# The queries' rotary columns, dealt by halves to two stationary tiles in the second stage

## What is computed

```python
def rope(x):                       # d = 32 columns, angle = position * inv
    x1, x2 = xf[..., : d // 2], xf[..., d // 2:]
    return concat([x1 * cos - x2 * sin, x2 * cos + x1 * sin])

q = (rms_norm(cq, mla_q_norm_w) @ mla_w_uq).reshape(B, S, 8, 64 + 32)
q_nope, q_rope = q[..., :64], rope(q[..., 64:])
kv = (rms_norm(ckv, mla_kv_norm_w) @ mla_w_ukv).reshape(B, S, 8, 64 + 64)
k_nope, v = kv[..., :64], kv[..., 64:]
scores = q_nope . k_nope + q_rope . rope(kr)      # kr is shared by the heads
```

## Time and profile before

| what | value |
|---|---|
| device time, median of 3 runs | 3495.73 us (3494.43 to 3495.84) |
| profiled execution, span from first to last instruction | 3494.4 us |
| TensorE (PE) busy | 3334.6 us, 95% |
| VectorE (DVE) busy | 2287.4 us, 65% |
| ScalarE (ACT) busy | 1631.7 us, 47% |
| GpSimd (POOL) busy | 934.6 us, 27% |
| mean granted TensorE clock | 0.976 of 2.4 GHz |

### The profile page before, as it was taken

How to read it: one execution, slowest core, us unless ns; L and a number is a source line. 1 busy time by engine, 2 the same in 40 slices (tenths; PEclk the granted TensorE clock), 3 DMA queues, 4 the chain that set the end, 5 groups by cost and what they waited for, 6 DMA issues and landing times. The chain is left out here.

```text
span 3494.4 us, 52272 instructions
## 1 busy us (share of the span) xinstructions
PE 3334.6 (95%) x19180; PEld 2879.2 (82%) x19180; DVE 2287.4 (65%) x3989; ACT 1631.7 (47%) x2115; POOL 934.6 (27%) x499
## 2 busy tenths in 40 slices
PE   7999979997999999999899589999999999999996
PEld 6888878885777777777688489999999999999995
DVE  5444447676888888887688855555555555555578
ACT  2111124443878777787444323333333333333476
POOL 0000000003888888888122101111111111111102
PEclk9999989998999999999899799999999999999998
DMA  4333346768133232220344245555555555555685
GB/s 153 114 114 114 117 168 236 264 242 230 32 73 71 60 73 47 47 45 14 125 154 158 103 136 175 174 173 166 165 168 174 173 168 165 166 174 174 211 273 203
DMA packets 350150, 506.17 MB, mean 145 GB/s; under 512 B 108369, under 2 KB 244305, under 8 KB 344769
## 3 DMA queue, kind: packets, MB, share of 16 engines
q1 hardware_dynamic: 336928, 457.39, 40.2%
q0 software_dynamic: 13088, 47.06, 5.7%
HBM read 366.03 MB, written 138.36 MB: 144 GB/s over the span
## 5 line engine op out<-in xcount | busy, mean ns | idle before, releaser
L64 PE MATMUL psum<-xeT_hi,w_hi 128*128 128x320 f32 x2048 | 634.4, 310 | 0.0
L66 PE MATMUL psum<-xeT_hi,w_lo 128*128 128x320 f32 x2048 | 632.8, 309 | 0.0
L65 PE MATMUL psum<-xeT_lo,w_hi 128*128 128x320 f32 x2048 | 632.8, 309 | 0.0
L2650 DVE TENSOR_TENSOR w_lo<-shared,w_hi 128x2048 fp32r<-128x2048 f32 x190 | 427.6, 2285 | 32.3 <-ACT w_hi L2485 32.3
L2485 ACT ACTIVATE w_hi<-shared 128x2048 fp32r<-128x2048 f32 x192 | 358.3, 1907 | 187.1 <-PE psum L66 187.1
L64 PEld LDWEIGHTS psum<-xeT_hi,w_hi 128*128 128x128 f32 x2048 | 384.5, 188 | 0.9
L65 PEld LDWEIGHTS psum<-xeT_lo,w_hi 128*128 128x128 f32 x2048 | 384.5, 188 | 0.6
L66 PEld LDWEIGHTS psum<-xeT_hi,w_lo 128*128 128x128 f32 x2048 | 384.5, 188 | 0.0
L1513 DVE TENSOR_REDUCE mx<-psum 128x1 f32<-128x1024 f32 x256 | 311.4, 1220 | 21.9 <-PE psum L1312 18.9
L2298 POOL DMA_INDIRECT xe<-x,idx_next x48 | 76.7, 1599 | 926.6 <-DVE gate_next L2682 860.1
L2714 DVE TENSOR_TENSOR h<-gated,psum 128x320 f32<-128x320 f32 x128 | 62.3, 487 | 331.7 <-PE psum L66 297.5
(11 more groups left out here) (436 smaller groups left out, 7826.0 us busy)
## 6 DMA issues: line engine op xcount, KB each, us to landing
shared<-in_w_gate SPq DMA_DIRECT2D x64, 1024.0 KB, 5.4
shared<-in_w_up SPq DMA_DIRECT2D x64, 1024.0 KB, 7.5
shared<-in_w_down SPq DMA_DIRECT2D x64, 1024.0 KB, 5.2
xT<-xaT SPq DMA_DIRECT2D x20, 1024.0 KB, 6.4
rec<-rec SPq DMA_DIRECT2D x20, 768.0 KB, 3.6
shared<-rec SPq DMA_DIRECT2D x20, 768.0 KB, 5.4
shared<-in_x SPq DMA_DIRECT2D x20, 512.0 KB, 4.9
cq_hi<-xT SPq DMA_DIRECT2D x20, 512.0 KB, 6.3
```

The costliest lines, as they stand in the source:

```text
L64: pe.matmul(out, a[0], b[0], start=first, stop=False)
L65: pe.matmul(out, a[0], b[1], start=False, stop=False)
L66: return pe.matmul(out, a[1], b[0], start=False, stop=last)
L2650: v.tensor_tensor(w_lo[n % 4][:], raw[n % 4], w_hi[n % 4][:].bitcast(F32), ALU.subtract).then_inc(s["lo_made"], 1)
```

## The change

The rotary columns are no longer kept with exchanged copies. The first halves (16 columns) of all eight heads make one stationary tile of 128 columns, the second halves another. A block then has two rotary items instead of four: "r0" in its step 0 and "r1" in its step 1; steps 2 and 3 have none, so that a block has 14 items. VectorE multiplies each by cosines and by sines and subtracts or adds; both results ("R0", "R1") are split and stored behind step 1. In DRAM the rotary rows lie as (half, head and column), so a head's 32 rows are two runs of 16, and every load of them has a source of 2 x 16 rows. The rotary tables come in 16 issues of 16 rows. Line 916 stays as it is.

```diff
+    HALF = KR // 2
+    ROT = MH * HALF
-    d["qr"] = nc.dram_tensor("qr", (2, MH * KR, T), F32, kind="Internal").ap()
+    d["qr"] = nc.dram_tensor("qr", (2, 2, MH * HALF, T), F32, kind="Internal").ap()
-        uq_hi, uq_lo = sb("uq_hi", [P, 2, D], F32R), sb("uq_lo", [P, 2, D], F32R)
+        uq_hi, uq_lo = (sb(n, [P, 2, MH * MN + 2 * ROT], F32R) for n in ("uq_hi", "uq_lo"))
...
-            return ["V", "K", "Q", "R" if step % 2 else "r"]
+            return ["V", "K", "Q"] + (["r0"], ["r1"], [], [])[step]
...
-                    for a in range(2):
-                        for g in range(4):
-                            sp.dma_start(cos_sin[b][KR * g:KR * (g + 1), a, :], d["rope_qT"][KR * a:KR * (a + 1), cols]
+                    for a, at in ((0, 0), (1, KR + HALF)):
+                        for g in range(MH):
+                            sp.dma_start(cos_sin[b][HALF * g:HALF * (g + 1), a, :], d["rope_qT"][at:at + HALF, cols]
...
-                    if u >= PREP0 + 1 and preps(u - 1)[1] % 2:
-                        store_pair(u - 1, "R")
+                    if u >= PREP0 + 1 and preps(u - 1)[1] == 1:
+                        store_pair(u - 1, "R0")
+                        store_pair(u - 1, "R1")
...
-                store_pair(LAST - 1, "R")
...
-                wait_stored(g, NT + 2, "R")
-                g.dma_start(q_hi[MN:KQ, first].bitcast(F32), d["qr"][0, 0:KR, first]).then_inc(c.head0_in, 16)
+                wait_stored(g, NT + 2, "R1")
+                g.dma_start(q_hi[MN:KQ, first].bitcast(F32), d["qr"][0, :, 0:HALF, first]).then_inc(c.head0_in, 16)
...
-                        at = step * P if what == "Q" else 512 + (step % 2) * 256 + (step // 2) * P
+                        at = step * P if what == "Q" else MH * MN + ROT * step
...
-                        prepare(u, kinds(preps(u)[1])[3])
+                        for what in kinds(preps(u)[1])[3:]:
+                            prepare(u, what)
...
+                        v.tensor_tensor(rotated[0], first_half, cos_sin[i % 2][:, 0, :], ALU.mult
+                        v.tensor_tensor(rotated[1], first_half, cos_sin[i % 2][:, 1, :], ALU.mult
...
+                        v.tensor_tensor(by_sin[:], second_half, cos_sin[i % 2][:, 1, :], ALU.mult
+                        v.tensor_tensor(by_cos[:], second_half, cos_sin[i % 2][:, 0, :], ALU.mult
+                        v.tensor_tensor(rotated[0], rotated[0], by_sin[:], ALU.subtract).then_inc(s["rope_summed"], 1)
+                        v.tensor_tensor(rotated[1], rotated[1], by_cos[:], ALU.add).then_inc(s["rope_summed"], 1)
...
-                        sp.dma_start(qT[b][w][MN:KQ, :].bitcast(F32), d["qr"][w, rot, :]).then_inc(arrived, 16)
+                        sp.dma_start(qT[b][w][MN:KQ, :].bitcast(F32), d["qr"][w, :, rot, :]).then_inc(arrived, 16)
...
-                    sp.dma_start(qT[0][0][MN:KQ, cols].bitcast(F32), d["qr"][0, 0:KR, cols]).then_inc(arrived, 16)
+                    sp.dma_start(qT[0][0][MN:KQ, cols].bitcast(F32), d["qr"][0, :, 0:KR // 2, cols]).then_inc(arrived, 16)
```

More of the change, by code:

```diff
@@ L552, in retention_backward_phase @@
         kr = [sb(f"kr_pair{b}", [KR, 2, P], F32R) for b in range(2)]
-        turned2 = sb("q_turned2", [P, 512])
+        by_cos, by_sin = (sb(n, [P, 512]) for n in ("q_by_cos", "q_by_sin"))
         pair2 = sb("pair2", [P, 2, 512], F32R)
@@ L567, in retention_backward_phase @@
         cos_sin = [krT[:, b * D:(b + 1) * D].rearrange("p (a n) -> p a n", a=2) for b in range(2)]
-        turned1 = krT[:, 2 * D:T]
+        rotated = [krT[:, 2 * D:T], sb("q_rotated1", [P, 512])[:]]
         raw = [krT[:, 0:W], krT[:, W:2 * W], early[3], early[4], early[1], raw_more[2], early[0], early[2]]
@@ L588, in retention_backward_phase @@
                  "lat_normed kr_turning kr_rotated lat_turned lat_hi_made lat_lo_made kr_hi_made kr_lo_made "
-                 "state_zeroed w_hi_made w_lo_made filled rope_turned pair_hi_made pair_lo_made rope_summed").split()
+                 "state_zeroed w_hi_made w_lo_made filled rope_by_cos rope_by_sin pair_hi_made pair_lo_made rope_summed").split()
         s = {n: c.sem("b_" + n) for n in names}
@@ L606, in kinds @@
         def kinds(step):
-            return ["V", "K", "Q", "R" if step % 2 else "r"]
+            return ["V", "K", "Q"] + (["r0"], ["r1"], [], [])[step]
         all_items = [(u, what) for u in range(PREP0, LAST) for what in kinds(preps(u)[1])]
         item_no = {key: n for n, key in enumerate(all_items)}
-        pair_no = {key: n for n, key in enumerate([key for key in all_items if key[1] != "r"])}
+        by_pair = []
+        for u, what in all_items:
+            by_pair += {"r0": [], "r1": [(u, "R0"), (u, "R1")]}.get(what, [(u, what)])
+        pair_no = {key: n for n, key in enumerate(by_pair)}
         def uq_parts(k, dst):
@@ L620, in uq_parts @@
                 for a in range(2):
-                    at = 512 + 256 * a + KR * hh
-                    parts.append((src[:, g, :, MN + KR * a:MN + KR * (a + 1)], dst[:, :, at:at + KR]))
+                    at = MH * MN + ROT * a + HALF * hh
+                    parts.append((src[:, g, :, MN + HALF * a:MN + HALF * (a + 1)], dst[:, :, at:at + HALF]))
             return parts
@@ L682, in load_cos_sin @@
                     if i >= 2:
-                        sp.wait_ge(s["rope_turned"], 4 * (i - 1))
+                        sp.wait_ge(s["rope_by_cos"], 2 * (i - 1))
+                        sp.wait_ge(s["rope_by_sin"], 2 * (i - 1))
                     b = i % 2
                     cols = slice((NB - 1 - i) * 512, (NB - i) * 512)
-                    for a in range(2):
-                        for g in range(4):
-                            sp.dma_start(cos_sin[b][KR * g:KR * (g + 1), a, :], d["rope_qT"][KR * a:KR * (a + 1), cols]
+                    for a, at in ((0, 0), (1, KR + HALF)):
+                        for g in range(MH):
+                            sp.dma_start(cos_sin[b][HALF * g:HALF * (g + 1), a, :], d["rope_qT"][at:at + HALF, cols]
                                          ).then_inc(cos_sin_in[b], 16)
@@ L697, in store_pair @@
                         dst = d["v"][:, 4 * tb + step].rearrange("a p n -> p a n")
-                    elif what == "R":
-                        dst = d["qr"][:, P * (step // 2):P * (step // 2 + 1), cols].rearrange("a p n -> p a n")
+                    elif what in ("R0", "R1"):
+                        dst = d["qr"][:, int(what == "R1"), :, cols].rearrange("a p n -> p a n")
                     else:
@@ L791, in prepare @@
                         u2, what2 = all_items[n - len(PREP_BANK)]
-                        if what2 in ("r", "R"):
-                            pe.wait_ge(s["rope_turned"], u2 - PREP0 + 1)
+                        if what2 in ("r0", "r1"):
+                            i2, a2 = preps(u2)
+                            pe.wait_ge(s["rope_by_cos"], 2 * i2 + a2 + 1)
+                            pe.wait_ge(s["rope_by_sin"], 2 * i2 + a2 + 1)
                         else:
@@ L940, in _ @@
                         split_hi(DK + 2 * u + 1)
[L941 to L945, removed]
+                    if prep and preps(u)[1] == 1:
+                        for part, what in enumerate(("R0", "R1")):
+                            m = pair_no[u, what]
+                            a.wait_ge(s["rope_summed"], 2 * preps(u)[0] + part + 1)
+                            wait_home(a, m)
+                            a.activation(pair[home[m]][:, 0, :], rotated[part], ACT.Copy).then_inc(s["pair_hi_made"], 1)
             @block.vector
@@ L1063, in _ @@
                         split_lo(DK + 2 * u + 1)
[L1064 to L1082, removed]
@@ new lines, in _ @@
+                    if prep and preps(u)[1] == 0:
+                        i = preps(u)[0]
+                        first_half = ps[:, prep_bank(item_no[u, "r0"]), :]
+                        v.wait_ge(s["filled"], item_no[u, "r0"] + 1)
+                        v.wait_ge(cos_sin_in[i % 2], 256 * (i // 2 + 1))
+                        if i >= 1:
+                            v.wait_ge(s["pair_hi_made"], pair_no[u - 3, "R1"] + 1)
+                            v.wait_ge(s["pair_lo_made"], pair_no[u - 3, "R1"] + 1)
+                        v.tensor_tensor(rotated[0], first_half, cos_sin[i % 2][:, 0, :], ALU.mult
+                                        ).then_inc(s["rope_by_cos"], 1)
+                        v.tensor_tensor(rotated[1], first_half, cos_sin[i % 2][:, 1, :], ALU.mult
+                                        ).then_inc(s["rope_by_sin"], 1)
@@ new lines, in _ @@
+                    if prep and preps(u)[1] == 1:
+                        i = preps(u)[0]
+                        second_half = ps[:, prep_bank(item_no[u, "r1"]), :]
+                        v.wait_ge(s["filled"], item_no[u, "r1"] + 1)
+                        wait_from_one(v, s["rope_summed"], 2 * i)
+                        v.tensor_tensor(by_sin[:], second_half, cos_sin[i % 2][:, 1, :], ALU.mult
```

(14 more changed lines are left out.)

## The result

The kernel became slower: 3512.24 us (3509.38 to 3513.77) against 3495.78 (3494.43 to 3500.13) for the kernel before on the same chip. The ratio is 1.0042, with a 95% interval of 1.0030 to 1.0054, or 14.7 us by the ratio; the two medians lie 16.5 us apart.

A forecast was written before the change was run, and what follows sets the result against it. TensorE was taken to bound the second stage's steps, transfers the way to attention. Steps and stall nearly cancel; the block ends 3.9 us later, of which 2.0 remain, plus 10.2 for uneven loads: +12.2, 3507.9 us; range 3494 to 3518.

The forecast's parts named there:

- Steps: Second stage: six removed rotary groups up to u = 16 save 1.40 us each, -8.4; the other four save 0.
- The stall: At u = 18 the unchanged wait for 16 items a block holds ScalarE, so TensorE's transposes wait: +8.1 us with the clock.
- SP's queue: At u = 20 sixteen table issues stand ahead of the stores, so V's store comes 3.0 us later.
- closing gap between the stores: Behind V's store at u = 20, a gap of some 0.8 us between stores closes and gives that back.
- Two engines: Rotary loads with a source of 2 by 16 rows are carried by two DMA engines instead of sixteen.
- (a): End of the block: GpSimd's last load, 64 KB on two engines, takes 1.7 us more.
- (c): Head 0's 256 and 320 KB rotary loads put 252 KB more on two engines, delaying the first score 10.2 us.
- step (b): Behind the block's end: loads follow the stores without a break, so only 2.0 of the 3.9 us delay remains.
- The first, sixteen engines: Rival for the rotary loads: spread over sixteen engines, they cost nothing extra; 3496.0, no change; chance 0.15.
- The second, no stall: Rival at u = 18: ScalarE isn't held, but loads still use two engines; 3499.5; chance 0.08.
- The third, neither: Rival: neither a stall at u = 18 nor loads on two engines; -7.7 us, 3488.0; chance 0.04.
- Later heads: Rival in attention: 14 loads each 5.7 us longer delay the maxima in seven heads, up to 40 us: 3548; chance 0.03.

The follow-up runs named there:

- all three faults mended: Kernel after with wait count 14, rotary loads as two of 16 rows each, and rotary tables issued a block earlier: 3490.18 us, 0.9980 of before.
- The kernel with halves: Kernel after with each rotary load made as two loads of 16 rows, nothing else changed: 3503.93 us, 1.0017 of before.
- the count: Kernel after with only ScalarE's wait changed from 16 to 14 items a block: 3503.45 us, 1.0017 of before.
- the columns: Kernel after with each rotary load cut into two by columns, source still 2 x 16 rows: 3512.43 us, 1.0039 of before.
- the tables alone: Kernel after with only the rotary tables of blocks 1 to 4 issued a block earlier: 3507.75 us, 1.0027 of before.

## Why the prediction was right, and where its terms were off

The sum put the kernel 12.2 us above the kernel before, at 3507.9; it came out 14.7 above by the ratio. Of the three parts of the sum, the steps up to u = 18 were put at -0.3 and measured -0.1, the way from u = 19 to the block's end at +3.9 and measured +4.6, and the way from there to the first score at +8.3 and measured +10.5. The mechanisms were those that were forecast; two sizes at the end were too small.

**Steps.** The six groups brought 1.4 us each, as worked out, and the four others nothing: the idle time at u = 20 grew from 2.01 to 3.38 us, by what the missing group at u = 19 left, and with all three faults mended the block still ends as long after the start of u = 19 as before (49.7 us, 49.6 before).

**The stall** is the term that came closest: 6.40 us measured for 6.3, 8.29 with the clock for 8.1. The high halves started 8.1 us into u = 18 (757.21), for 8.0 worked out, and from there to the turned key 6.2 us passed (to 763.41), for 6.1; at u = 14 nothing waited. Both runs on the wait say that the count is its whole cause: corrected, the stall is gone; put into the kernel before, it costs 9.9 us. That is 1.6 more than 8.3; its trace shows 0.7 more than 8.3 in u = 18 and another 1.6 up to the block's end, and no run tells what holds it up there.

**SP's queue.** 16 issues took 8.01 us and V's store came 3.0 us later, as predicted. The block's end moved 4.6 us instead of 3.9, although GpSimd's last load took only 1.3 us more, for 1.7. What was too small is the part ahead of that load: it was issued 47.6 us after the start of u = 19 (820.58) instead of 44.4 (820.46), 3.2 later and not 2.2. The 0.8 us that a closing gap between the stores was to give back did not come. What I had not worked out is that this term alone is worth 3 to 4.5 us of the result: I expected the loads behind it to take back half of the later block's end.

**Two engines.** That a source of 2 x 16 rows is carried by two of sixteen engines, which the trace of before could only bound, is what the stretches show: a share of 0.11 to 0.13, where two of sixteen are 0.125. The same loads in halves leave the share near 1, and cut by columns they don't. The packets say it too. The hardware queue has 416 more of them (336928 before). 40 more loads of tables, each with 16 ends, are 640 more; 16 rotary loads on this queue with 2 ends instead of 16 are 224 fewer; the difference is 416. The kernel with halves bears this reading out. Its 32 rotary loads with 16 ends each would be 256 more than the 16 before, 896 with those of the tables, and that is its difference from before (the first row is the kernel before, the second the one with halves):

```profile
q1 hardware_dynamic: 336928, 457.39, 40.2%
...
q1 hardware_dynamic: 337824, 457.40, 40.7%
```

For GpSimd's last load, on another queue, only the landing (6.1 us for 4.8, and 4.5 in halves) speaks for two engines; its packets were not read in this way.
The rule of the Trainium skill, "DMA: Bandwidth & Descriptors", section "Why a DMA increments its semaphore by 16 and not by 1", that the split is the largest count up to 16 which divides the slowest dimension of both sides, gives 2 for this source; share and packets agree with it. That the destination has 32 rows didn't help.

**The sizes at the end of the block.** This is where most of the shortfall lies: from the block's end to the score 10.5 us instead of 8.3. All of it is the landing of one store. From the block's end to the store of the maxima 10.6 us pass in either kernel (825.74 to 836.34 and 827.21 to 837.80), and from the issue of the row's read to the score 4.7 and 4.6; in between the store took 15.3 us instead of 4.8. Parts (a) and (c), the two engines, were put at 11.9 together; the run with halves brought 9.7, at the price of one more issue on GpSimd and one more on SP per load (about 0.5 us each in the traces), so by estimate some 10 to 11. They were not too small.

That (c) came out near its 10.2 is in part luck. It gave each of the two engines 25.3 GB/s. They ran alone for 14.4 us, at 42 GB/s, so some 21 each:

```profile
838.20:852.60 14.40, 3.78 (x8) 2.34 (x8) 4.61 (x4) 0.00 (x0) 3.43 (x4) 0.50 0.13 42
```

This cost no more because the other loads were through sooner: the share falls 11.0 us behind the block's end (838.2), where it fell 13.5 behind it before (839.2).

What failed is step (b): the loads were to start at 829.1 in the kernel before, 3.4 us behind the block's end, and in the changed one 1.6 behind it, which was to hide 1.9 of the 3.9 us. A finer view of before shows that the loads had begun sooner, and one of after that nothing flows at first:

```profile
825.70:827.20 1.50, 1.46 (x4) 1.20 (x5) 0.23 (x1) 1.28 (x1) 1.44 (x2) 0.50 1.08 414
827.20:828.70 1.50, 1.50 (x5) 1.07 (x4) 1.50 (x2) 0.00 (x0) 1.44 (x2) 0.50 1.13 358
...
827.20:828.20 1.00, 0.99 (x2) 0.81 (x3) 0.00 (x0) 1.00 (x1) 0.94 (x2) 0.50 0.00 0
```

In the second of these stretches the rate falls below the 404 to 414 GB/s of the stores, so loads are among the transfers by then. I had read the start from a stretch that I began at 829.10, where the rate is the loads' alone. In the kernel before, the stores' tail thus covers the first 1.5 us or more behind the block's end; in the kernel after, nothing moves for the first 1.0 us (the last row), and of the delay nothing is seen to be hidden. With sixteen engines the score is even 1.1 to 1.4 us further from the block's end than before, not 1.9 closer; the additional issues of the halves have a part in that, which no run separates.

**The rivals.** The first, sixteen engines, was priced at 3496; the run that makes it true took 6.6 us more than before. It had the loads flow 0.3 us later, and the score came 5.3 later. Of these 5.0 us, 1.7 lie ahead of the block's end, which was 3.9 later and not 2.2 (SP's queue, above), and 3.3 behind it: 1.9 by step (b), the rest where the additional issues of the halves lie. The second, no stall, was priced at 3499.5, 3.8 above before; the run took 6.2 above. The third, neither, was put at 3488.0, a gain of 7.7; the run gained 3.0, and only with the tables earlier too did it gain 7.1. Later heads pay nothing that the time behind the first score shows (2648.6 us before, 2649.8 after), though each of their loads is as uneven as head 0's.

**Not foreseen.** Unit 8 waited 4.92 us for head 0's rotary rows. It costs nothing by itself, as TensorE then waits 13.59 us for the row of maxima anyway.

## What to carry to other kernels

A count written as a number in a wait belongs to the loop that it counts: when the items of a block become fewer, the wait asks for later work, and the profile shows it as an engine that stands still with its own inputs ready. The outer size of a load's source decided here how many DMA engines carry it, two for 2 x 16 rows, and a store of 2 KB behind such loads on the same queue landed only when they were through; cutting each load so that its pieces have sixteen rows in their outer dimension costs one more issue and gave back 8.3 us here. And before a delay is called hidden, the transfers around it should be read in stretches as fine as the delay itself: a stretch that is put where the rate looks clean tells nothing about when it began.

## What the runs showed of the hardware

- Two DMA engines alone carried 31 GB/s (840.00 to 846.00) to 48 GB/s (847.00 to 852.60), 16 to 24 each; the stores reached 25.3 per engine with sixteen at work (404 GB/s).
- The store of 2 KB from 128 rows took 15.3 to 16.3 us behind the uneven loads in four traces (the kernel after, the count, the columns, the tables alone), and 6.1 behind the same loads in halves.
- After 6.40 us without work TensorE ran at a granted clock of 0.50, its 1.2 GHz level, in the stretch from its first transpose to 767.20, and at 1.00 from there to the step's end; that gap and the slower matmuls behind it together made 8.3 us:

```profile
763.50:767.20 3.70, 3.69 (x13) 3.50 (x14) 3.70 (x7) 1.22 (x5) 0.00 (x0) 0.50 0.90 256
767.20:773.00 5.80, 5.80 (x30) 5.23 (x28) 4.74 (x19) 1.77 (x6) 0.00 (x0) 1.00 0.87 333
```
